# Attention stage of a two-layer trunk: token-stationary queries and keys, turned by transfers and VectorE

## What is computed

```python
qkv = (x @ w_qkv).reshape(bsz, seqlen, 3, 16, 128)
q, k, v = qkv[:, :, 0], qkv[:, :, 1], qkv[:, :, 2]
q = _partial_rope(q, cos, sin) * 128 ** -0.5     # rotates channels 0:16 with 16:32 of each head
k = _partial_rope(k, cos, sin)
s_own = jnp.where(k_pos <= q_pos, q @ k.T, NEG_INF)     # per head
o = softmax(s_own) @ v
y = o.reshape(bsz, seqlen, 2048) @ w_out
x = layer_norm(alpha * x + y)
```

## Time and profile before

| | before |
|---|---|
| median of 3 runs (2097.20 to 2097.58) | 2097.36 us |
| the profiled execution | 2096.86 us |
| its span, first to last instruction | 2095.0 us |
| PE busy | 2085.9 us, 100% |
| DVE busy | 1290.4 us, 62% |
| ACT busy | 975.1 us, 47% |
| DMA queue of SP | 432.79 MB, 65.2% of the 16 engines' span |
| DMA queue of ACT | 5.77 MB, 0.7% |
| DMA rate | 209 GB/s mean |

### The profile page before, as it was taken

How to read it: one execution, slowest core, us unless ns; L and a number is a source line. 1 busy time by engine, 2 the same in 40 slices (tenths; PEclk the granted TensorE clock), 3 DMA queues, 4 the chain that set the end, 5 groups by cost and what they waited for, 6 DMA issues and landing times.

```text
span 2095.0 us, 28820 instructions
## 1 busy us (share of the span) xinstructions
PE 2085.9 (100%) x9918; PEld 1749.5 (84%) x9918; DVE 1290.4 (62%) x1246; ACT 975.1 (47%) x1172; POOL 21.3 (1%) x16
## 2 busy tenths in 40 slices
PE   9999999999999999999999999999999999999999
PEld 8898888888888888888988888888888888888887
DVE  6869666665555565555766667675665554555565
ACT  5596455434444443443644445454434443443442
POOL 0000010000000000000000000010000000000000
PEclk9999999999999999999999999999999999999999
DMA  7665758766766766775654556658666766766763
GB/s 257 195 197 189 235 180 261 250 200 203 236 222 183 238 230 201 219 233 171 193 186 158 168 167 225 202 189 267 216 210 212 241 206 195 243 218 228 241 212 120
DMA packets 233547, 439.80 MB, mean 210 GB/s; under 512 B 15056, under 2 KB 37840, under 8 KB 232432
## 3 DMA queue, kind: packets, MB, share of 16 engines
q1 hardware_dynamic: 232032, 432.79, 65.2%
q10 hardware_dynamic: 1424, 5.77, 0.7%
HBM read 419.63 MB, written 18.87 MB: 209 GB/s over the span
## 4 chain that ended last, share of the span: by engine, by line
PE 99%; DMA 0%; ACT 0%; issue 0%; DVE 0%; ACTq 0%
PE ps L427 75%; PE ps L419 11%; PE ps L416 5%; PE ps L726 1%; PE ps L725 1%; PE ps L724 1%; PE ps L558 1%; PE ps L739 0%; DMA wst<-in_rg_w_in_dram 0%; PE ps L524 0%; PE ps L523 0%; PE ps L525 0%; PE ps L596 0%; PE ps L714 0%; PE ps L599 0%; PE ps L575 0%
## 5 line engine op out<-in xcount | busy, mean ns | idle before, releaser
L1014 DVE TENSOR_TENSOR wl<-wst,wh 128x1024 fp32r<-128x1024 f32 x743 | 887.8, 1219 | 327.3 <-ACT wh L757 324.0
L757 ACT ACTIVATE wh<-wst 128x1024 fp32r<-128x1024 f32 x743 | 769.8, 1059 | 649.1 <-PE ps L427 411.8
L427 PE MATMUL ps<-wh,hid 128*128 128x512 f32 x2560 | 695.9, 390 | 0.0
L427 PEld LDWEIGHTS ps<-wh,hid 128*128 128x128 f32 x2560 | 479.5, 188 | 98.9
L427 PE MATMUL ps<-wh,xin 128*128 128x512 f32 x2048 | 548.9, 389 | 0.0
L427 PEld LDWEIGHTS ps<-wh,xin 128*128 128x128 f32 x2048 | 383.9, 188 | 79.4
L427 PE MATMUL ps<-wl,hid 128*128 128x512 f32 x1280 | 404.6, 389 | 0.0
L419 PE MATMUL ps<-xin,wh 128*128 128x512 f32 x960 | 331.2, 395 | 0.8 <-DVE wl L1014 0.8
L427 PE MATMUL ps<-wl,xin 128*128 128x512 f32 x1024 | 315.2, 389 | 0.0
L427 PEld LDWEIGHTS ps<-wl,hid 128*128 128x128 f32 x1280 | 240.2, 188 | 50.0
L416 PE MATMUL ps<-xin,wl 128*128 128x256 f32 x960 | 256.8, 278 | 0.0
(11 more groups left out here) (138 smaller groups left out, 835.9 us busy)
## 6 DMA issues: line engine op xcount, KB each, us to landing
wst<-in_mlp_w_dram SPq DMA_DIRECT2D x512, 512.0 KB, 4.7
wst<-in_moba_w_qkv_dram SPq DMA_DIRECT2D x96, 512.0 KB, 4.6
wst<-in_rg_w_in_dram SPq DMA_DIRECT2D x62, 512.0 KB, 4.1
wst<-in_rg_w_out_dram SPq DMA_DIRECT2D x32, 512.0 KB, 4.9
sq_by_quad<-f SPq DMA_DIRECT2D x128, 128.0 KB, 2.5
f<-sq_by_quad SPq DMA_DIRECT2D x32, 512.0 KB, 5.1
wst<-in_moba_w_out_dram SPq DMA_DIRECT2D x32, 512.0 KB, 5.3
f<-in_x_dram SPq DMA_DIRECT2D x8, 256.0 KB, 6.3
```

Of the source, the lines that this page charges most:

```text
L427: return pe.matmul(banks(half)[:, a, :], src[:, c, part, a * P:(a + 1) * P], (wl if low else wh)[:, s, w], start=(c == 0 and part + low == 0),
L757: act.activation(wh[:, off % SPLITS, :], wst[:, slot, :], ACT.Copy).then_inc(wh_done, 1)
L1014: dve.tensor_tensor(wl[:, off % SPLITS, :], wst[:, off % STAGE, :], wh[:, off % SPLITS, :], ALU.subtract).then_inc(wl_done, 1)
```

## The change

Q and K turns take the form `token_turn`. Their results go the way of the MLP's squares but from SBUF to SBUF: ACT evicts them permuted into `qk_out`, sixteen DMAs of 32 partitions by 1 KB carry the rectangles into `qk_quad` (eight issued by SP, eight by ACT), and DVE transposes the 32x32 squares into `qg` or `kg`, then rotates as before. The softmax weights are divided by DVE in the permuted order into `prob_out`, moved in the same way (1.5 KB rows, sixteen DMAs), and transposed by DVE; PE's transposes and ACT's copies of them go. The softmax and the weighted sums of a group are put off into the next group's Q and K turns, and for the last group into the output projection, whose first two turns are now interleaved by `W2_ORDER`. PSUM banks 0 to 3 hold the turns, 4 to 7 the scores and sums. The scores stand ahead of V's last block. The loops over groups are written out on every engine. The first turn uses the begun token form that the MLPs have.

The core of the diff, with the new calls (most waits and the renamed arguments cut):

```diff
+MOVES = 16 * GROUP * GROUP
+PV_AT = BLOCKS
+        qk_out = f2[:, 0:1024].rearrange("p (q n) -> p q n", q=GROUP)
+        qk_quad = f3[:, 3072:4096].rearrange("p (i n) -> p i n", i=GROUP)
+        prob_out = f2[:, 1536:3072].rearrange("p (q n) -> p q n", q=GROUP)
+        prob_quad = f2[:, 0:1536].rearrange("p (i n) -> p i n", i=GROUP)
+        def part_moves(dst, src, of):
+            return [(dst[q * 32:(q + 1) * 32, i, :], src[i * 32:(i + 1) * 32, q, :])
+                    for i in of for q in range(GROUP)]
```

SP:

```diff
+            def move_qk(g, part):
+                sp.wait_ge(qk_evict, HALVES * (2 * g + part + 1))
+                if 2 * g + part:
+                    sp.wait_ge(qk_ready, 2 * g + part)
+                for dst, src in part_moves(qk_quad, qk_out, (0, 1)):
+                    sp.dma_start(dst, src).then_inc(qk_moved, 16)
+            def move_p(g):
+                sp.wait_ge(p_ready, g + 1)
+                for dst, src in part_moves(prob_quad, prob_out, (0, 1)):
+                    sp.dma_start(dst, src).then_inc(p_moved, 16)
+            for g in range(NG):
+                k_before = {2: lambda: move_qk(g - 1, 1)} if g else {}
+                p_before = {BLOCKS - 1: lambda: move_p(g - 1)} if g else {}
+                for part, also in enumerate((k_before, p_before, {2: lambda: move_qk(g, 0)})):
+                    load_turn(moba_w_qkv[0], part * D + g * COLS, B_QKV + (3 * g + part) * BLOCKS, also)
             load_rows(1)
-            with sp.Fori(0, NG) as t:
+            for n, (t, kb) in enumerate(W2_ORDER):
+                if n == 2:
+                    move_qk(NG - 1, 1)
+                if n == 2 * BLOCKS - 1:
+                    move_p(NG - 1)
+                load_block(cols_of(moba_w_out[0], t * COLS)[kb], n, B_MO + n)
+            with sp.Fori(2, NG) as t:
                 load_turn(moba_w_out[0], t * COLS, B_MO + t * BLOCKS)
```

PE, the loop over groups:

```diff
+            for g in range(NG):
+                own, other = 2 * (g % 2), 2 * (1 - g % 2)
+                if g == 0:
+                    begun_token_turn(1, b, R_LN1)
+                else:
+                    token_turn(xin, own, b, R_LN1)
+                token_turn(xin, other, b + BLOCKS, R_LN1, {1: lambda: weighted(g - 1)} if g else {})
+                token_turn(xin, own, b + 2 * BLOCKS, R_LN1, {BLOCKS - 1: lambda: scores(g)})
```

PE, the output projection:

```diff
+                if n == 2:
+                    held_pair(hid, b, ready, free, {HELD: lambda: pe.wait_ge(bias_ready, NG),
+                                                     PV_AT: lambda: weighted(NG - 1)})
```

ACT, the loop over groups:

```diff
+                if g:
+                    exponentials(g - 1)
+                splits(b, no, START, START + 2)
+                if g:
+                    move_p(g - 1)
+                splits(b, no, START + 2, LATE + 1)
+                take_qk(g, 0, own)
+                splits(b, no, LATE + 1, NEXT)
+                b, no = b + BLOCKS, no + 1
+                splits(b, no, START, START + 1)
+                if g:
+                    weighted_hi(g - 1)
+                splits(b, no, START + 1, LATE + 1)
+                take_qk(g, 1, other)
+                splits(b, no, LATE + 1, NEXT)
```

DVE, the loop over groups:

```diff
+                if g:
+                    splits(b, START, START + 2)
+                    softmax_end(g - 1)
+                    splits(b, START + 2, LATE)
+                    turn_p(g - 1)
+                    splits(b, LATE, NEXT)
...
+                b += BLOCKS
+                splits(b, START, START + 2)
+                rotate(g, 1, kg)
+                splits(b, START + 2, START + 3)
+                rotated(g, 1, kg)
+                splits(b, START + 3, LATE + 1)
+                dve.wait_ge(scores_done, g + 1)
```

DVE, the output projection:

```diff
+                    if n == 2 and t == 0:
+                        splits(b, START, START + 2)
+                        softmax_end(NG - 1)
+                        prepare(n - 1, t)
+                        splits(b, START + 2, LATE)
+                        turn_p(NG - 1)
+                        splits(b, LATE, LATE + 2)
+                        weighted_lo(NG - 1)
+                        splits(b, LATE + 2, LATE + held)
```

More of the change, by code:

```diff
@@ L438, in token_turn @@
                             for a in range(HALVES):
-                                mm = token_step(src, half, a, c, part, low)
+                                mm = token_step(src, first, a, c, part, low)
                     mm.then_inc(mm_done, 1)
@@ L452, in last_token_turn @@
                             for part, low in ((0, 0), (1, 0), (0, 1)):
[L453 removed]
+                                mm = token_step(hid, 4, a, c, part, low)
                         if a == 1:
@@ new lines, in take_qk @@
+            def take_qk(g, part, first):
+                act.wait_ge(mm_done, B_QKV + (3 * g + part + 1) * BLOCKS)
+                if part == 0 and g:
+                    act.wait_ge(pt_ready, g)
+                if part:
+                    act.wait_ge(qk_moved, MOVES * (2 * g + 1))
+                for a in range(HALVES):
+                    by_part = qk_out.rearrange("p q (c a r) -> p a c q r", c=GROUP, a=HALVES)[:, a]
+                    by_col = ps[:, first + a, :].rearrange("p (c q r) -> p c q r", c=GROUP, q=GROUP)
+                    act.activation(by_part, by_col, ACT.Copy).then_inc(qk_evict, 1)
+                act.wait_ge(qk_evict, HALVES * (2 * g + part + 1))
+                if 2 * g + part:
+                    act.wait_ge(qk_ready, 2 * g + part)
+                for dst, src in part_moves(qk_quad, qk_out, (2, 3)):
+                    act.dma_start(dst, src).then_inc(qk_moved, 16)
@@ new lines, in exponentials, with move_p @@
+            def exponentials(g):
+                act.wait_ge(bias_ready, g + 1)
+                for h in range(GROUP):
+                    for a, cols in enumerate((slice(0, P), slice(P, 3 * P))):
+                        ex = act.activation(prob[:, h, cols], prob[:, h, cols], ACT.Exp, scale=QK_SCALE,
+                                            bias=stat[:, h, 2 + a:3 + a], accum_out=stat[:, h, 4 + a:5 + a])
+                ex.then_inc(exp_done, 1)
+            def move_p(g):
+                act.wait_ge(p_ready, g + 1)
+                for dst, src in part_moves(prob_quad, prob_out, (2, 3)):
+                    act.dma_start(dst, src).then_inc(p_moved, 16)
@@ new lines, in weighted_hi @@
+            def weighted_hi(g):
+                act.wait_ge(pv_done, g + 1)
+                act.activation(hid[:, g * GROUP:(g + 1) * GROUP, 0, :],
+                               ps[:, 6:8, :].rearrange("p b (c t) -> p (b c) t", t=T), ACT.Copy).then_inc(pv_hi, 1)
+            for g in range(NG):
+                b, no = B_QKV + 3 * g * BLOCKS, B_QKV // BLOCKS + 3 * g
+                own, other = 2 * (g % 2), 2 * (1 - g % 2)
+                if g:
[13 more added lines that the diff above has]
+                splits(b, no, LATE + 1, NEXT)
+                b, no = b + BLOCKS, no + 1
+                splits(b, no, START, LATE + 1)
+                act.wait_ge(mm_done, b + BLOCKS)
+                act.activation(vg, ps[:, own:own + 2, :], ACT.Copy).then_inc(v_stored, 1)
+                splits(b, no, LATE + 1, NEXT)
```

317 lines of the change are left out of this document (135 added, 182 removed).

## The result

| | before | after |
|---|---|---|
| median, us | 2097.28 (2097.13 to 2097.58, 4 runs) | 2117.14 (2112.36 to 2120.53, 4 runs) |
| profiled execution, us | 2096.86 | 2112.36 |
| span, us | 2095.0 | 2110.6 |
| granted clock, mean | 1.0 | 0.996 |

The ratio is 1.0092 (95%: 1.008 to 1.0105): the changed kernel is slower, by 19.9 us between the medians. The forecast was 2090.3, faster. In the table of the experiments one execution of e11 is left out, a slow one of 2986.64 us at a mean granted clock of 0.654.

A forecast was written before the change was run, and what follows sets the result against it. PE was taken to bound the kernel, with 99% of the chain. The terms -11.0 + 2.8 + 1.1 = -7.1 us, taken from the median of 2097.36, gave 2090.3 us, with a range of 2086.0 to 2100.0.

The forecast's parts named there:

- Part 3: K's moves and rotation: PE waits 0.7 us with the semaphore ahead of the scores, +2.8 us for four groups.
- Part 4: Softmax weights' moves and transpose: hidden behind K's first block; only the last group's PE wait counts, +1.1 us.
- Parts 1 and 2: Attention stage: token form of Q and K turns -4.4, twelve PE transposes a group gone -7.0, resumed turns +0.4: -11.0 us.
- part 1: Q and K turns in token form take 21.76 us: seven lose 0.49 each, the begun first turn 1.0; -4.4 us.
- The start: SP's and ACT's moves of K begin at K's eviction, 1.3 us after V's turn starts.
- Q's path has no date: Rotated Q is wanted only with K, a turn later, so its moves and rotation were given no date.
- The issue: Each move of K on SP and ACT takes 0.51 us to issue, eight take 4.0 us.
- The bound of part 3: Wait ahead of the scores at most 3 us a group, +12, with issues of 0.6 us and a landing of 6.2.
- The 1.8 to spare: Transposed softmax weights ready at 22.7 us after Q's turn starts, PE asks at 24.5, so 1.8 us to spare.
- rival (c): SP's and ACT's issues take turns at one generator, so moves come late: +20.5, 2117.9 us; chance 0.12.
- rival (b): Issues of 0.6 us make PE's waits eat the gain: 2095.4 us, +2.9 at the far end; chance 0.13.

The follow-up runs named there:

- e11: The changed kernel without the eight DMAs that ACT issues for each move, SP's eight kept; 2099.31 us.
- e1: The changed kernel with none of the sixteen moves of Q, K and the softmax weights issued; 2085.84 us.
- e3: The changed kernel with DVE's transpose and rotation of K ahead of the split of V's offset 10; 2097.09 us.
- e10: The changed kernel without the eight DMAs that SP issues for each move, ACT's eight kept; 2099.74 us.
- e5: e3's kernel with the weighted sums placed one block later; 2090.56 us.
- e7: e5's kernel with the two 1 MB loads of gain and bias rows issued ahead of group 2; 2093.50 us.
- e9: e8's kernel with the gain and bias rows loaded at the head of group 2's K weights; 2085.80 us.
- e2: The changed kernel with the same sixteen DMAs for each move, each carrying a quarter of the row; 2115.64 us.
- e8: e7's kernel with ACT's eight DMAs of each move issued by POOL; 2087.88 us.
- e12: e9's kernel with POOL issuing twelve of the sixteen DMAs of each move and SP four; 2101.76 us.

## Why the prediction was wrong, point by point

The steps that failed are the dates of parts 3 and 4, and a term that was not there: PE's waits came to 18.6 us where the sum had 3.9, and the lower clock that came with them, 7.8 us, stood in no line.

**Parts 1 and 2 were right**, as a sum: -11.0 predicted, -11.5 measured (e1). A token turn takes the 21.76 of part 1 there. In the profiled execution the first matmul of the stage is at 1002.05 and the first of V's turn in group 0 at 1047.45. With one token turn of 21.76 taken off, that leaves 23.64 for the begun first turn, the number that was predicted. The rule of the Trainium skill that was weighed there (TensorE: Matmul & The Clock Gate, Back-to-back issue gap) would, by an estimate of 0.1 us a turn from the form, have made parts 1 and 2 about -7.4, and the kernel without moves 2090.0; the measured -11.5 stands against it.

**Part 3 had the mechanism and missed its size.** The wait is the predicted one, ended by the predicted add, and the load behind SP's moves was the last link (e3). The terms:
- The start. The eight issues on SP were dated by K's eviction. But SP's queue is in order and has two loads of weights ahead of the moves, each waiting for a buffer of DVE's, and DVE is late there because it has just rotated Q. This is the sentence "Q's path has no date": Q itself is not wanted early, but its moves and its rotation shift the queues that carry K's. It cost 1.5 us in group 2; in group 0 SP's first move goes out 4.6 after V's start.
- The issue. 0.51 us each was taken from four moves with nothing beside them. Between starts it is 0.6, and with the slower ones among them eight take 5.0 to 6.0 on SP and 5.0 to 6.2 on ACT. That is 1 to 2 us a group. The other queue is not the reason: in e11, where ACT issues none, SP's eight take 4.9 to 5.8, and in e10 ACT's take 5.0 to 5.5. It is these moves that cost more than the moves of squares. From e11's timeline, SP in group 1:

```profile
1124.86 4.96 SPq L370 DMA_DIRECT2D f<-f  x8
```

- The rows. In group 3 the moves stand behind 2 MB of gain and bias rows, and land in up to 7.5; this was priced at nothing. Of the wait of 4.1 there, 1.8 is left in e3 and e5, and it goes when the rows are moved (e7, e9).

In all, 12.5 us of wait ahead of the scores where the sum had 2.8. The bound of part 3, +12 at "issues of 0.6 us and a landing of 6.2", was reached and a little passed, but not by its own conditions: the issues were 0.6, the load of group 2 landed in 4.1 (only group 3's, behind the rows, in 6.6), and the rest came from SP's late start and the rows. The issue was judged from a row of other moves, 128 KB each to DRAM.

**Part 4 had the date wrong.** In group 0 the moves of the softmax weights are issued from 1092.49, 14.4 after Q's turn started at 1078.1 (12.8 predicted). ACT issues for 6.1 us and then has three splits to do before DVE can transpose. The timelines of after for ACT and DVE:

```profile
1092.49 6.11 ACTq L1008 DMA_DIRECT2D f<-f  x8
1098.70 3.91 ACT L754 ACTIVATE wh<-wst 128x1024 fp32r<-128x1024 f32 x4 [9.73 <-issue]
...
1103.21 1.77 DVE L1351 STREAM_TRANSPOSE f<-f 128x1536 f32<-128x1536 f32 x1
```

The weights are there at 26.9 where 22.7 was predicted; PE asks at 24.5. The 1.8 to spare were smaller than the errors of two terms, and I gave that case no chance of its own. In groups 1 and 2 the moves start at the predicted date (13.0 in group 1), the longer issuing uses up what was to spare, and PE waits 0.2. Waits of 6.1 in all, for the predicted 1.1.

**A term was missing.** No line of the sum had the lower clock behind a wait, and rival (c) hadn't either. It is 7.8 of the 26.9 us.

The profiled execution is 2112.36 for a predicted 2089.8, so 22.6 over: 18.6 - 3.9 = 14.7 of waits, 7.8 of clock, -0.35 since parts 1 and 2 brought a little more, and 0.4 that I can't place. The median is another 4.8 higher; the executions at 2116 to 2121 have a mean granted clock of 0.993 to 0.994 and not 0.996, so more of the lower level; their waits were not traced.

**The rivals.** Rival (c) gave 2117.9, and the time is 2117.14, but that is a coincidence of numbers: its mechanism was two queues that take turns at one generator, with the moves themselves late. Both queues issue at 0.6 at the same time and SP no faster alone (e11), the moves land in 2.6 in the median, and e3 recovers 20 us with every move in place. Its sentence from the Trainium skill (DMA: Bandwidth & Descriptors, Rules for kernel authors: below 64 KB a transfer is mostly overhead) agrees with e2, where a quarter of the bytes took the same time (2115.64 against 2117.14). Its other half, that two transfers to disjoint halves of the partitions serialize, did not set the time of these small moves: in e9 the sixteen of group 1's softmax weights land one every 0.25 us, as fast as both queues issue them, each 2.0 to 2.8 after its issue, so several are under way at once. What happened is rival (b), issues of 0.6 us, for which 2095.4 was given with its far end at +2.9, plus what its sum left out: SP's late start, the rows, the softmax weights of the first group, and the clock.

**What stays open.** How much of the price of SP's half and of ACT's lies in the issuing and how much in what each delays behind it isn't separated: e10 and e11 only show that each half alone costs about 14 over e1 and both 31. And what sets group 0's remaining wait was not tried on its own; it is 2.1 in e3, 0.25 in e5, 1.0 in e7, 1.5 in e8 and gone in e9, with no edit between them that bears on it but ACT's moves going to POOL.

## What to carry to other kernels

Price a DMA that is moved onto an engine's queue as an instruction of that engine, 0.5 to 0.6 us for each of the kind here (a quarter of the bytes changed nothing), and then follow what stands behind it in that queue; look also at what stands in front, since a queue in order starts them only when its older waits are over. Place small transfers that someone waits for ahead of the large ones, on every queue: an engine that is free early sends its large loads in front of another's small ones. And where PE is the bound, a wait of some microseconds should be priced with what may follow it at half clock.

## What the runs showed of the hardware that was not expected

- **The clock falls in or behind a wait of 2 us and more, but not with each.** PE's scores after a wait of 3.4 us (group 2 of after), from the timeline:

```profile
1223.10 1.06 PE L631 MATMUL ps<-f 128*128 128x256 f32 x2
1223.95 0.63 PE L630 MATMUL ps<-f 128*128 128x128 f32 x2
1224.38 1.06 PE L631 MATMUL ps<-f 128*128 128x256 f32 x2
```

  A pair takes 1.06 and 0.63 here. The weighted sums of group 3, which have the same tiles, run at 0.60 and 0.38 right behind a wait of 3.2 us, at a granted clock of 1.00:

```profile
1332.43 0.70 PE L640 MATMUL ps<-f 128*128 128x256 f32 x2 [3.00 <-DVE f L1351]
1332.97 0.38 PE L641 MATMUL ps<-f 128*128 128x128 f32 x2
1333.19 0.60 PE L640 MATMUL ps<-f 128*128 128x256 f32 x2
```

  Over all runs, no wait under 1.9 us was followed by the lower level. Of those from 2.0 to 5.3 us most were, for 3 to 6 us behind the wait, and six not (2.1, 2.8, 2.9, 3.1, 3.2, 3.7). What tells them apart isn't known from these runs.
- **POOL issues as well as the others.** Its moves stand 0.49 us apart, against 0.6 on SP and ACT, and land in 2.5. In the kernel before it was idle in this stage, so its queue was the free place.
- **Enough large transfers issued just ahead of a small one delay its landing**, from whichever queue they come. Behind two loads of 512 KB, issued in the 1.6 us before, the moves of after's group 2 landed in 3.2 to 4.5 us; behind three (e12) in 4.8 to 5.9; behind 2 MB of rows and two weight loads (e3's group 3) in 5.8 to 7.6. The median of all is 2.6.
